# Softmax attention of a two-block network: 36 single-parity steps against 19 steps that take both parities

## The chip, the cores and the metric

The kernel runs on one core of one Trainium2 chip. The metric is the device time of one execution in microseconds. All five engines of the core take part: TensorE (PE) does the products, VectorE (DVE) and ScalarE (ACT) the elementwise work, GpSimd (POOL) the low halves of the weights, SyncE (SP) starts the transfers.

## The reference, cut to what matters

The network is a first block of two layers and a second block of one, over 512 tokens of width 1024. The change touches one stage of the first block, which runs once in each of its two layers: the projection to the 3072 columns `dn_qkv` with its short causal convolution and SiLU, and beside it the softmax attention with a sliding window over 16 query heads and 2 key heads of width 64.

```python
dn_qkv = jax.nn.silu(causal_dwconv(dn_qkv, dn_conv[l]))      # 3072 columns, 4 taps

# swa_sink_attention, in 4 blocks of 128 queries; each sees its own and the previous block of keys
s = jnp.einsum('bnqhgd,bnkhd->bnhgqk', qb, kb) * (D ** -0.5)
s = jnp.where(mask[None, :, None, None], s, -jnp.inf)
m = jnp.maximum(jnp.max(s, axis=-1, keepdims=True), sink)
p = jnp.exp(s - m)
denom = jnp.sum(p, axis=-1, keepdims=True) + jnp.exp(sink - m)
o = jnp.einsum('bnhgqk,bnkhd->bnqhgd', p / denom, vb)
```

## The kernel before, in words

Weights come in slabs of two tiles of 128 columns. For each tile ACT makes a rounded high half (`high`, line 212) and POOL the remainder (`low`, line 216), and `gemm` (line 269) multiplies both with the high and low halves of the activations: 24 matmuls of 512 columns for a tile, 12 of them for the first four depth chunks and 12 for the rest. `high` of tile t + 2 waits until tile t is multiplied. The tiles of this stage take the PSUM banks 0, 1 and 2 in turn.

The stage has 24 such tiles (`QKV_TILES`). VectorE's `conv(t)` reads the finished tile out of its bank in four instructions of 512 columns (lines 971 and 974); it waits for the end of `gemm` of tile t. ScalarE's `silu` follows in groups, after tiles 3, 7, 11, 15 and 19 and at the end.

Between the halves of the tiles lie the steps of the attention. A unit `u` is two query heads of one parity (their 64 rows stand on partitions 0 to 63 or 64 to 127) in one block of queries: 32 units, the first 8 with one block of keys (narrow, 128 columns a head), the other 24 with two (wide, 256 columns a head). A unit goes through

- PE `scores` (line 874): two products into bank 4 or 5, contraction over 64 partitions;
- DVE `before`: scale and mask (line 928), row maximum (932), maximum with the sink, difference, negation (935 to 938);
- ACT `exps` (991, 993): two exponentials with their sums, and the sink's;
- DVE `after`: sum, reciprocal, two scalings (943, 945, 949);
- PE `turn` (885): 2 or 4 transposes into bank 6; ACT `copies` (999) reads them out;
- PE `values` (898): 2 or 4 products with 64 output rows, into bank 3 or 7 (`values_bank`, which alternates with the pair of heads);
- once both parities of a pair are there: ACT `store` (1004) keeps the high half, DVE `keep` (955) the low half, which frees the bank (`a_done`).

Step `u` of PE issues scores of `u`, turn of `u - 3` and values of `u - 4`. ACT's step is exps, copies, store; DVE's is keep, before, after. Each engine works through its own written order, so what a waiting instruction has behind it waits too. `slots(t)` places three steps in two tiles: after the first and the second half of an even tile and after the first half of an odd one; 36 steps in all. On DVE a step after the first half of tile t stands ahead of `conv(t)`, one after the second half stands behind it; on ACT `high(t + 2)` lies between.

The PSUM bank of a pair's values is guarded by

```python
elif u % 2 == 0 and u >= 4:
    pe.wait_ge(a_done, u // 2 - 1)
```

SP's queue loads the remaining slabs of this stage, writes zeros to two arrays in DRAM, and loads the first slabs of the next stage. The stage ends with a barrier of all engines.

Of the kernel before, what the change touches and what calls it, by code (L numbers as in the profile page):

```python
# [12 lines left out]
ACT = mybir.ActivationFunctionType  # L13
# [117 lines left out]
def build(nc, d, out):  # L131
# [4 lines left out]
    with ExitStack() as ctx:  # L136
# [274 lines left out]
        with ExitStack() as st:  # L411
# [147 lines left out]
            with nc.Fori(0, DEPTH) as l:  # L559
# [253 lines left out]
                def values_bank(w):  # L813

                    return ps[7 if w % 2 else 3]

                def stored(w):
                    i, m = w // 4, 2 * (w % 4)
                    return (slice(m, m + 2), slice(i * P, (i + 1) * P),
                            values_bank(w)[:, 0:2 * P].rearrange("p (m t) -> p m t", m=2))  # L820

                NU, LAG, QKV_TILES, SILU = 8, 3, 24, 4
                units = NU * TT

                def width(u):

                    return P if u < NU else 2 * P

                def s1(u):
                    return big[:, 24 + u % 4, :]  # L830

                def turned(u):
                    return big[:, 28 + u % 2, :]

                def st_(u, n, w=2):
                    return big[:, 30, 16 * (u % 4) + 2 * n:16 * (u % 4) + 2 * n + w]

                def two(ap, u):

                    return ap[:, 0:2 * width(u)].rearrange("p (j k) -> p j k", j=2)  # L840

                def slots(t):

                    first = 3 * (t // 2) + (2 if t % 2 else 0)
                    return (first,) if t % 2 else (first, first + 1)

                with nc.Block() as block:  # L847
                    @block.sync
# [16 lines left out]

                    @block.tensor
                    def _(pe):
                        def scores(u):
                            i, w, par = u // NU, u % NU // 2, u % 2
                            if u >= 2:  # L870
                                pe.wait_ge(a_pre, 5 * (u - 2) + 1)
                            for j in range(2):
                                m = 2 * w + j
                                ins = nc.tensor.matmul(ps[4 + u % 2][:, width(u) * j:width(u) * (j + 1)],
                                                       sq[HD * par:HD * par + HD, m, i * P:(i + 1) * P],
                                                       kd[HD * par:HD * par + HD, m // 4, (i + 2) * P - width(u):(i + 2) * P],
                                                       start=True, stop=True)
                            ins.then_inc(a_scored, 1)

                        def turn(u):  # L880
                            pe.wait_ge(a_post, u + 1)
                            if u >= 1:
                                pe.wait_ge(a_tc, u)
                            for n in range(2 * width(u) // P):
                                ins = nc.tensor.transpose(ps[6][:, n * P:(n + 1) * P], s1(u)[:, n * P:(n + 1) * P], ident)
                            ins.then_inc(a_tp, 1)

                        def values(u):
                            i, w, par, nb = u // NU, u % NU // 2, u % 2, width(u) // P
                            pe.wait_ge(a_tc, u + 1)  # L890
                            if u == 0:
                                pe.wait_ge(evacuated[3], use[G_SO + 3])
                            elif u % 2 == 0 and u >= 4:
                                pe.wait_ge(a_done, u // 2 - 1)
                            for j in range(2):
                                g, c0 = (2 * w + j) // 4, P * j
                                for b in range(nb):
                                    ins = nc.tensor.matmul(values_bank(u // 2)[HD * par:HD * par + HD, c0:c0 + P],
                                                           vs[:, i + 2 - nb + b, HD * g:HD * g + HD],
                                                           turned(u)[:, (nb * j + b) * P:(nb * j + b + 1) * P],  # L900
                                                           start=(b == 0), stop=(b == nb - 1))
                            ins.then_inc(a_out, 1)

                        def step(u):
                            if u < units:
                                scores(u)
                            if LAG <= u < units + LAG:
                                turn(u - LAG)
                            if LAG < u <= units + LAG:
                                values(u - LAG - 1)  # L910

                        for t in range(QKV_TILES):
                            gemm(pe, G_QKV + t, (hh, hl), k1=4)
                            step(slots(t)[0])
                            gemm(pe, G_QKV + t, (hh, hl), k0=4)
                            if t % 2 == 0:
                                step(slots(t)[1])

                    @block.vector
                    def _(dve):  # L920
                        def before(u):

                            w, par = u % NU // 2, u % 2
                            dve.wait_ge(a_scored, u + 1)
                            if u >= 4:
                                dve.wait_ge(a_tp, u - 3)
# [31 lines left out]
                        def step(u):  # L958
                            if u >= LAG + 3 and u % 2 == 0:
                                keep((u - LAG - 3) // 2)  # L960
                            if u < units:
                                before(u)
                            if 2 <= u < units + 2:
                                after(u - 2)

                        def conv(t):
                            gt = G_QKV + t
# [8 lines left out]
                                                               ).then_inc(c_tap if s < 3 else evacuated[bank[gt]], 1)  # L976

                        for t in range(QKV_TILES):
                            step(slots(t)[0])
                            conv(t)  # L980
                            if t % 2 == 0:
                                step(slots(t)[1])
                        keep(units // 2 - 1)

                    @block.scalar
                    def _(act):
# [7 lines left out]

                        def copies(u):
                            act.wait_ge(a_tp, u + 1)
                            if u >= 2:
                                act.wait_ge(a_out, u - 1)
                            nc.scalar.activation(turned(u)[:, 0:2 * width(u)], ps[6][:, 0:2 * width(u)], ACT.Copy).then_inc(a_tc, 1)

                        def store(w):
                            m, t, bank_ = stored(w)
                            act.wait_ge(a_out, 2 * w + 2)
                            nc.scalar.activation(o_swa[0][:, m, t], bank_, ACT.Copy).then_inc(a_high, 1)

                        def step(u):
                            if u < units:
                                exps(u)
                            if LAG <= u < units + LAG:
                                copies(u - LAG)  # L1010
                            if LAG < u <= units + LAG and (u - LAG - 1) % 2 == 1:
                                store((u - LAG - 1) // 2)

                        def silu(t):
                            gt = G_QKV + t
# [3 lines left out]
                        high(act, G_QKV)  # L1019
                        high(act, G_QKV + 1)  # L1020
                        for t in range(QKV_TILES):
                            step(slots(t)[0])
                            high(act, G_QKV + t + 2)
                            if t % 2 == 0:
                                step(slots(t)[1])
# [1811 lines left out]
```

## Time and profile before

| | us |
|---|---|
| median of 3 runs (3077.69 to 3086.43) | 3082.3 |
| the profiled execution, its own time | 3085.06 |
| its span in the profile | 3083.2 |
| PE busy in the span | 2745.9 (89%) |
| DVE busy | 1411.5 (46%) |
| ACT busy | 1110.3 (36%) |
| POOL busy | 902.1 (29%) |

The mean granted clock of TensorE is 0.936 of full speed. Times in rows are microseconds from the start of the span unless marked ns. PEld is the load of stationary weights, which overlaps the products. A matmul of plain f32 operands shows as two records; one of the rounded halves and a transpose show as one. The end of a matmul's record is modelled, so that records overlap; the distance from one start to the next is the measure of what a product costs. "idle before <- X" names what the engine waited for.

### The profile page before, as it was taken

What the parts mean: (1) busy time and instruction counts of PE and PEld (TensorE: products, weight loads), DVE (VectorE), ACT (ScalarE), POOL (GpSimd) and SP (SyncE); (2) the same over time, 40 slices, a digit from 0 to 9 for tenths busy, and PEclk for the clock granted to TensorE, in tenths of its full rate; (3) what the DMA queues carried; (4) which work ended last, traced back from release to release, by engine and by line L of the source; (5) the groups of instructions that cost most, each with busy time, mean ns of one, the idle gap of its engine ahead of it and who ended that gap; (6) DMA issues with size and microseconds to landing.
All of it is one profiled execution on the core that took longest, in us unless ns stands there. A gap on an engine that the chain in (4) does not pass through costs nothing. (4 is left out here: it accounts for less than half of the span.)

```text
span 3083.2 us, 34820 instructions
## 1 busy us (share of the span) xinstructions
PE 2745.9 (89%) x12993; PEld 2174.7 (71%) x12993; DVE 1411.5 (46%) x2693; ACT 1110.3 (36%) x1896; POOL 902.1 (29%) x402
## 2 busy tenths in 40 slices
PE   2789999898979999658999989998999987998998
PEld 1567768797858878536776778876788775875676
DVE  4247747654623430233775576453343108624423
ACT  1335455235333321033454532443333213224423
POOL 0342222111424444214222211133344332321242
PEclk6899999899989999869999989999999998988999
DMA  5211313644212322332113265422222225521132
GB/s 171 82 55 55 110 62 108 166 147 143 83 55 96 98 94 93 100 116 69 55 55 110 69 161 178 140 93 68 82 95 95 89 87 135 130 69 35 41 116 82
DMA packets 347832, 299.79 MB, mean 97 GB/s; under 512 B 56910, under 2 KB 335652, under 8 KB 346660
## 3 DMA queue, kind: packets, MB, share of 16 engines
q1 hardware_dynamic: 295716, 279.49, 29.3%
q10 hardware_dynamic: 51968, 18.35, 2.3%
q8 instruction: 90, 1.47, 0.2%
q14 instruction: 58, 0.48, 0.0%
HBM read 267.89 MB, written 29.93 MB: 97 GB/s over the span
## 5 line engine op out<-in xcount | busy, mean ns | idle before, releaser
L269 PE MATMUL ps<-hh,split 128*128 128x512 f32 x3936 | 1352.2, 410 | 97.0 <-POOL split L216 50.5
L216 POOL TENSOR_TENSOR split<-ring,split 128x1024 fp32r<-128x1024 f32 (+2 forms) x342 | 798.6, 2336 | 1724.6 <-ACT split L212 1724.6
L269 PEld LDWEIGHTS ps<-hh,split 128*128 128x128 f32 x3936 | 755.6, 192 | 284.8 <-POOL split L216 71.7
L269 PE MATMUL ps<-hl,split 128*128 128x512 f32 x1968 | 783.0, 398 | 0.0
L212 ACT ACTIVATE split<-ring 128x1024 fp32r<-128x1024 f32 (+2 forms) x342 | 348.4, 1020 | 934.2 <-PE ps L269 719.6
L269 PEld LDWEIGHTS ps<-hl,split 128*128 128x128 f32 x1968 | 379.3, 193 | 74.9 <-issue 7.4
L269 PE MATMUL ps<-split 128*128 128x512 f32 x1152 | 286.4, 406 | 13.0 <-PEq L847 11.1
L269 PEld LDWEIGHTS ps<-split 128*128 128x128 f32 x1152 | 219.3, 191 | 75.0 <-issue 26.8
L1883 PE MATMUL ps<-split 128*128 128x512 f32 x1056 | 243.4, 393 | 9.6 <-PEq L1762 9.6
L1883 PEld LDWEIGHTS ps<-split 128*128 128x128 f32 x1056 | 200.8, 190 | 52.2 <-issue 10.4
L457 DVE SCALAR_TENSOR_TENSOR vs<-ring,c_act,vs 128x256 f32<-128x256 f32 x336 | 179.5, 534 | 6.3
L554 POOL TENSOR_TENSOR split<-ring,split 128x1024 fp32r<-128x1024 f32 x32 | 76.2, 2381 | 361.3 <-ACT split L546 361.3
L991 ACT ACTIVATE big<-big 128x256 f32<-128x256 f32 (+1 forms) x128 | 60.7, 475 | 179.3 <-DVE big L938 179.2
L1896 DVE SCALAR_TENSOR_TENSOR x<-ps,mod,x 128x512 f32 x16 | 12.0, 751 | 234.8 <-PE ps L1883 234.8
L974 DVE SCALAR_TENSOR_TENSOR big<-ps,pv,big 128x511 f32<-128x511 f32 x144 | 107.8, 749 | 5.1
L1807 DVE TENSOR_TENSOR wk<-wk,ps 128x512 f32<-128x512 f32 x44 | 30.3, 688 | 163.3 <-PE ps L269 163.3
L1796 DVE TENSOR_SCALAR wk<-ps,pv 128x512 f32<-128x512 f32 x44 | 33.1, 751 | 111.9 <-PE ps L269 111.9
L475 PE MATMUL ps<-cst,vs 128*128 128x1 f32 x192 | 32.5, 273 | 56.7 <-DVE vs L457 56.2
L971 DVE TENSOR_SCALAR big<-ps,pv 128x512 f32<-128x512 f32 x48 | 36.0, 751 | 91.5 <-PE ps L269 91.5
L475 PEld LDWEIGHTS ps<-cst,vs 128*128 128x128 f32 x192 | 34.6, 238 | 60.9 <-DVE vs L457 57.4
L1799 DVE SCALAR_TENSOR_TENSOR wk<-ps,pv,wk 128x511 f32<-128x511 f32 x88 | 65.9, 749 | 13.7 <-DVE wk L1796 6.2
L1097 DVE TENSOR_TENSOR big<-big,wk 128x512 f32<-128x512 f32 x32 | 39.2, 1225 | 71.4 <-ACT wk L1079 71.4
(370 smaller groups left out, 3339.7 us busy)
## 6 DMA issues: line engine op xcount, KB each, us to landing
ring<-in_w_in_dram SPq DMA_DIRECT2D x60, 1024.0 KB, 5.2
ring<-in_w_up_dram SPq DMA_DIRECT2D x44, 1024.0 KB, 5.1
ring<-in_w_ada_dram SPq DMA_DIRECT2D x64, 512.0 KB, 3.6
ring<-in_w_in_dram SPq DMA_DIRECT2D x34, 512.0 KB, 5.3
ring<-in_w_ada_dram SPq DMA_DIRECT2D x16, 1024.0 KB, 5.3
ring<-in_w_down_dram SPq DMA_DIRECT2D x16, 896.0 KB, 4.7
ring<-in_w_swa_out_dram SPq DMA_DIRECT2D x8, 1024.0 KB, 5.0
ring<-in_w_dn_out_dram SPq DMA_DIRECT2D x8, 1024.0 KB, 5.1
```

The lines of the kernel that those rows point to most:

```text
L212: nc.scalar.activation(halves(pt, nk)[0], slot(n, nk)[:, :, e * P:(e + 1) * P], ACT.Copy).then_inc(high_made, 1)
L216: on.tensor_tensor(halves(pt, nk)[1], slot(n, nk)[:, :, e * P:(e + 1) * P], halves(pt, nk)[0], ALU.subtract).then_inc(low_made, 1)
L269: ins = nc.tensor.matmul(ps[bank[gt]][0:m, :], w[:, k, :], r[:, k, :], start=(k == 0 and w is w_high and r is rhs[0]), stop=(k == nk - 1 a ...
L457: nc.vector.scalar_tensor_tensor(out=acc, in0=w, scalar=c_act[:, k:k + 1], in1=acc, op0=ALU.mult, op1=ALU.add).then_inc(ada_added, 1)
L475: ins = nc.tensor.matmul(out[:, e:e + 1], ada_sum[:, m % 2, e * P:(e + 1) * P], ones[:, 0:1], start=True, stop=True)
L554: nc.gpsimd.tensor_tensor(halves(gt, KD)[1], quarter((gt - G_GB) % 2, KD), halves(gt, KD)[0], ALU.subtract).then_inc(low_made, 1)
L971: nc.vector.tensor_scalar(y, tile[:, :], w[3], None, ALU.mult).then_inc(c_tap, 1)
L974: nc.vector.scalar_tensor_tensor(out=y[:, s:], in0=tile[:, 0:T - s], scalar=w[3 - s], in1=y[:, s:], op0=ALU.mult, op1=ALU.add).then_inc(c_ ...
L991: nc.scalar.activation(half, half, ACT.Exp, bias=st_(u, 2)[:, j:j + 1], accum_out=st_(u, 3)[:, j:j + 1]).then_inc(a_exp, 1)
L1097: nc.vector.tensor_tensor(tile, tile, wk[:, 10 + n % 2, :], ALU.mult).then_inc(n_scaled, 1)
L1799: nc.vector.scalar_tensor_tensor(out=y[:, s:], in0=ps_[:, 0:T - s], scalar=w[2 - s], in1=y[:, s:], op0=ALU.mult, op1=ALU.add).then_inc(u_t ...
L1883: ins = nc.tensor.matmul(ps[bank[gt]][:, :], w[:, k, :], r[:, k0 + k, :], start=(k0 + k == 0 and w is w_high and r is g_high), stop=(k0 + ...
```

## The change

A step now takes both parities of a pair of heads (a double, `v`), 16 doubles in place of 32 units. Within `scores` and `values` the products alternate between the parities, that is, between the two halves of the array: of its rows in `scores` (banks 4 and 5), of its columns in `values`. All values go to bank 3. `turn` writes its transposes to bank 6 or 7 by parity. There are 6 buffers of scores and 4 of turned scores in place of 4 and 2. `LAG` is 2 doubles: step `v` is scores of `v`, turn of `v - 2`, values of `v - 3`. On ACT the copies of the step lead its exponentials; on DVE the order is keep, after (of the double before), before. 19 steps are spread over the 48 halves of tiles: after halves 0, 2, 5, 7, 10, 12, 15, 17 and so on to 45, where an odd number is the end of a tile. The guard of bank 3 is `a_done` of the double before, and that `keep` now stands in DVE's step of the same number as the `values` that waits for it.

```diff
-                NU, LAG, QKV_TILES, SILU = 8, 3, 24, 4
-                units = NU * TT
+                NU, LAG, QKV_TILES, SILU = 8, 2, 24, 4
+                doubles = NU * TT // 2
-                def slots(t):
-                    first = 3 * (t // 2) + (2 if t % 2 else 0)
-                    return (first,) if t % 2 else (first, first + 1)
+                def slots(t, half):
+                    steps = doubles + LAG + 1
+                    return [v for v in range(steps) if v * 2 * QKV_TILES // steps == 2 * t + half]
...
+                        def scores(v):
+                            i, w, n = v // 4, v % 4, width(2 * v)
+                            if v >= 1:
+                                pe.wait_ge(a_pre, 5 * (2 * v - 1) + 1)
                             for j in range(2):
                                 m = 2 * w + j
+                                for par in range(2):
+                                    ins = nc.tensor.matmul(ps[4 + par][:, n * j:n * (j + 1)],
+                                                           sq[HD * par:HD * par + HD, m, i * P:(i + 1) * P],
+                                                           kd[HD * par:HD * par + HD, m // 4, (i + 2) * P - n:(i + 2) * P],
+                                                           start=True, stop=True)
+                                    if j:
+                                        ins.then_inc(a_scored, 1)
+                        def turn(v):
+                            pe.wait_ge(a_post, 2 * v + 2)
+                            if v >= 1:
+                                pe.wait_ge(a_tc, 2 * v)
+                            for u in (2 * v, 2 * v + 1):
+                                for n in range(2 * width(u) // P):
+                                    ins = nc.tensor.transpose(ps[6 + u % 2][:, n * P:(n + 1) * P], s1(u)[:, n * P:(n + 1) * P], ident)
+                                ins.then_inc(a_tp, 1)
+                        def values(v):
+                            i, w, nb = v // 4, v % 4, width(2 * v) // P
+                            pe.wait_ge(a_tc, 2 * v + 2)
+                            if v == 0:
                                 pe.wait_ge(evacuated[3], use[G_SO + 3])
+                            else:
+                                pe.wait_ge(a_done, v)
...
                                 for b in range(nb):
+                                    for par in range(2):
+                                        ins = nc.tensor.matmul(ps[3][HD * par:HD * par + HD, c0:c0 + P],
...
-                        def step(u):
-                            if u >= LAG + 3 and u % 2 == 0:
-                                keep((u - LAG - 3) // 2)
-                            if u < units:
-                                before(u)
-                            if 2 <= u < units + 2:
-                                after(u - 2)
+                        def step(v):
+                            if LAG + 2 <= v:
+                                keep(v - LAG - 2)
+                            if 1 <= v <= doubles:
+                                after(2 * v - 2)
+                                after(2 * v - 1)
+                            if v < doubles:
+                                before(2 * v)
+                                before(2 * v + 1)
...
+                            if LAG <= v < doubles + LAG:
+                                copies(2 * (v - LAG))
+                                copies(2 * (v - LAG) + 1)
+                            if v < doubles:
+                                exps(2 * v)
+                                exps(2 * v + 1)
+                            if LAG < v <= doubles + LAG:
+                                store(v - LAG - 1)
```

## Rows read from the trace of the kernel before

**Rows 1.** The page's busy time, share of the span and instructions, by engine.
```profile
PE 2745.9 (89%) x12993; PEld 2174.7 (71%) x12993; DVE 1411.5 (46%) x2693; ACT 1110.3 (36%) x1896; POOL 902.1 (29%) x402
```

**Rows 2.** Windows, both layers' stage; length, busy PE, PEld, DVE, ACT, POOL; clock, DMA.
```profile
195.77:418.49 222.72, 218.22 (x1040) 162.60 (x1040) 151.70 (x395) 102.39 (x260) 57.23 (x24) 0.99 0.24 76
1455.08:1677.84 222.76, 218.25 (x1040) 162.70 (x1040) 151.72 (x395) 102.39 (x260) 57.21 (x24) 0.99 0.24 76
```

**Rows 3.** Timeline of PE: a tile, a wide step, half a tile; start, length, records.
```profile
280.77 0.50 PE L269 MATMUL ps<-hh,split 128*128 128x512 f32 x1
...
286.46 1.13 PE L874 MATMUL ps<-kd,sq 64*128 64x256 f32 x4
287.51 0.66 PE L885 MATMUL ps<-cst,big 128*128 128x128 f32 x4
288.10 1.09 PE L898 MATMUL ps<-big,vs 128*64 128x128 f32 x8
289.12 0.50 PE L269 MATMUL ps<-hh,split 128*128 128x512 f32 x1
...
292.06 1.13 PE L874 MATMUL ps<-kd,sq 64*128 64x256 f32 x4
```

**Rows 4.** Timeline of PE, one narrow step.
```profile
230.96 0.71 PE L874 MATMUL ps<-kd,sq 64*128 64x128 f32 x4
231.60 0.44 PE L885 MATMUL ps<-cst,big 128*128 128x128 f32 x2
231.97 0.65 PE L898 MATMUL ps<-big,vs 128*64 128x128 f32 x4
232.55 0.50 PE L269 MATMUL ps<-hh,split 128*128 128x512 f32 x1
```

**Rows 5.** Timeline of PE in the second block, products that alternate between halves.
```profile
2652.44 2.67 PE L2231 MATMUL ps<-b_uc,b_drive_w 128*64 128x64 f32 x84
...
2681.53 0.66 PE L2248 MATMUL ps<-b_w_c,b_read_w 64*128 64x63 f32 x8
2682.12 0.66 PE L2243 MATMUL ps<-b_uc,x 128*128 128x64 f32 x4
2682.71 0.66 PE L2248 MATMUL ps<-b_w_c,b_read_w 64*128 64x63 f32 x8
```

**Rows 6.** Waits of PE in the first layer's stage: us in total, times, longest.
```profile
PE ps L885 <- ACT big L999: 4.2, 7, 1.2
```

**Rows 7.** Timeline of DVE: a wide unit's before and after, a tile's conv, a keep.
```profile
287.62 0.69 DVE L928 SCALAR_TENSOR_TENSOR big<-ps,cst 128x512 f32<-128x512 f32 x1 [0.67 <-PE ps L874]
...
289.41 0.15 DVE L943 TENSOR_TENSOR big<-big 128x2 f32<-128x2 f32 x1
...
289.80 0.61 DVE L949 TENSOR_SCALAR big<-big 128x256 f32<-128x256 f32 x2
...
292.17 0.75 DVE L971 TENSOR_SCALAR big<-ps,pv 128x512 f32<-128x512 f32 x1 [1.76 <-PE ps L269]
...
295.19 0.42 DVE L955 TENSOR_TENSOR split<-ps,split 128x256 fp32r<-128x256 f32 x1
```

**Rows 8.** Timeline of ACT: a silu group between its tables, then exps, copy, store.
```profile
265.21 1.28 ACT L1017 ACT_TABLE_LOAD   x1
...
268.70 1.28 ACT L991 ACT_TABLE_LOAD   x1
...
289.54 0.51 ACT L991 ACTIVATE big<-big 128x256 f32<-128x256 f32 x1 [4.63 <-DVE big L938]
...
290.63 0.58 ACT L999 ACTIVATE big<-ps 128x512 f32<-128x512 f32 x1
291.11 0.37 ACT L1004 ACTIVATE split<-ps 128x256 fp32r<-128x256 f32 x1
```
**Rows 9.** Windows around an idle time of PE in the second block; columns as in Rows 2.
```profile
2932.03:2935.38 3.35, 0.00 (x0) 0.03 (x1) 1.93 (x2) 1.15 (x2) 1.26 (x1) 1.00 0.03 7
2935.38:2938.79 3.41, 3.41 (x8) 2.76 (x9) 2.06 (x3) 0.00 (x0) 0.00 (x0) 0.50 0.90 305
```

More of the change, by code:

```diff
@@ L811, in build, with stored @@
                 zeros = big[:, 30:32, :].rearrange("p a c -> p (a c)")[:, 2 * P:2 * P + ZERO]
[L813 to L818, printed above, removed]
+                def stored(v):
+                    i, m = v // 4, 2 * (v % 4)
                     return (slice(m, m + 2), slice(i * P, (i + 1) * P),
[L820 to L823 removed]
+                            ps[3][:, 0:2 * P].rearrange("p (m t) -> p m t", m=2))
+                NU, LAG, QKV_TILES, SILU = 8, 2, 24, 4
+                doubles = NU * TT // 2
                 def width(u):
@@ L873, in scores @@
                                 m = 2 * w + j
[L874 to L891, printed above, removed]
+                                for par in range(2):
[5 more added lines that the diff above has]
+                                        ins.then_inc(a_scored, 1)
@@ L897, in values @@
                                 for b in range(nb):
[L898 to L901, printed above, removed]
-                            ins.then_inc(a_out, 1)
-                        def step(u):
-                            if u < units:
[L906 to L910, printed above, removed]
+                                    for par in range(2):
+                                        ins = nc.tensor.matmul(ps[3][HD * par:HD * par + HD, c0:c0 + P],
+                                                               vs[:, i + 2 - nb + b, HD * g:HD * g + HD],
+                                                               turned(2 * v + par)[:, (nb * j + b) * P:(nb * j + b + 1) * P],
+                                                               start=(b == 0), stop=(b == nb - 1))
+                            ins.then_inc(a_out, 1)
+                        def step(v):
+                            if v < doubles:
+                                scores(v)
+                            if LAG <= v < doubles + LAG:
+                                turn(v - LAG)
+                            if LAG < v <= doubles + LAG:
+                                values(v - LAG - 1)
                         for t in range(QKV_TILES):
                             gemm(pe, G_QKV + t, (hh, hl), k1=4)
-                            step(slots(t)[0])
+                            for v in slots(t, 0):
+                                step(v)
                             gemm(pe, G_QKV + t, (hh, hl), k0=4)
-                            if t % 2 == 0:
-                                step(slots(t)[1])
+                            for v in slots(t, 1):
+                                step(v)
                     @block.vector
@@ L978, in _ @@
                         for t in range(QKV_TILES):
-                            step(slots(t)[0])
+                            for v in slots(t, 0):
+                                step(v)
                             conv(t)
-                            if t % 2 == 0:
-                                step(slots(t)[1])
-                        keep(units // 2 - 1)
+                            for v in slots(t, 1):
+                                step(v)
+                        keep(doubles - 1)
                     @block.scalar
@@ L996, in copies, with step @@
                             act.wait_ge(a_tp, u + 1)
-                            if u >= 2:
-                                act.wait_ge(a_out, u - 1)
-                            nc.scalar.activation(turned(u)[:, 0:2 * width(u)], ps[6][:, 0:2 * width(u)], ACT.Copy).then_inc(a_tc, 1)
+                            if u >= 4:
+                                act.wait_ge(a_out, u // 2 - 1)
+                            nc.scalar.activation(turned(u)[:, 0:2 * width(u)], ps[6 + u % 2][:, 0:2 * width(u)], ACT.Copy
+                                                 ).then_inc(a_tc, 1)
                         def store(w):
                             m, t, bank_ = stored(w)
-                            act.wait_ge(a_out, 2 * w + 2)
+                            act.wait_ge(a_out, w + 1)
                             nc.scalar.activation(o_swa[0][:, m, t], bank_, ACT.Copy).then_inc(a_high, 1)
[L1006 to L1012, printed above, removed]
+                        def step(v):
+                            if LAG <= v < doubles + LAG:
+                                copies(2 * (v - LAG))
+                                copies(2 * (v - LAG) + 1)
+                            if v < doubles:
+                                exps(2 * v)
+                                exps(2 * v + 1)
+                            if LAG < v <= doubles + LAG:
+                                store(v - LAG - 1)
                         def silu(t):
@@ L1021, in _ @@
                         for t in range(QKV_TILES):
-                            step(slots(t)[0])
+                            for v in slots(t, 0):
+                                step(v)
                             high(act, G_QKV + t + 2)
-                            if t % 2 == 0:
-                                step(slots(t)[1])
+                            for v in slots(t, 1):
+                                step(v)
                             if t % SILU == SILU - 1 and t + 1 < QKV_TILES:
```

19 lines of the change are left out of this document (6 added, 13 removed).

## The prediction, before the run

> **What bounds the kernel now.** I read the page first: PE is busy for 89% of the span and no other engine for half of it [rows 1]. Then the windows of the stage that the change touches. It lasts 222.7 us in each layer, 445.5 us in all, at a granted clock of 0.99; PE is busy for 218.2 of the 222.7, DVE for 151.7, ACT for 102.4 [rows 2]. So the stage is a queue of products, and what counts is how long PE's program takes and what it waits for. The table of waits names one wait of PE inside it: turns that wait until ACT has copied the transposes before them, 4.2 us in 7 times [rows 6]. The reader should see that whatever else is on DVE and ACT is at present covered.
>
> The timeline of PE gives the prices by distance of starts. A tile with a step behind it takes 286.46 - 280.77 = 5.69 us and half a tile 292.06 - 289.12 = 2.94, so a bare half is 2.75, a tile 5.50, and the passage into and out of a step costs 0.19. A wide step takes 1.05 for scores, 0.59 for turn and 1.02 for values, 2.66 together [rows 3]; a narrow one 0.64 + 0.37 + 0.58 = 1.59 [rows 4].
>
> **Products of two halves.** The trace of before has no attention product that alternates, but the second block has products that do. At L2231 84 records of 64 columns, alternating between the column halves, take 2.67 us, 0.22 of it the tail of the last: 0.03 us a record. At L2248, alternating between the row halves, eight records of 63 columns take 2682.12 - 2681.53 = 0.59 us, 0.07 a record, while the whole-array products at L2243, with as many columns, need 2682.71 - 2682.12 = 0.59 for four, 0.15 a record [rows 5]. Values in one half take 1.02 / 8 = 0.13 a record of 128 columns [rows 3], which is four times 0.03 for twice the columns. Both point to two halves at work at once. I bound the price of a pair by that of one product (full overlap) and that of two (none), and take the first, since the two nearest rows both show it. In between: if the two records of a product must pass before the other half joins, each group ends half a product later, 0.26 for wide scores and 0.13 for values, about 10 us over both layers.
>
> **PE's work after.** A wide double: scores 1.05 (four products in the time of two), turn with 8 transposes, values 1.02. Four transposes take 0.59 and two 0.37 [rows 3, 4], so one more is 0.11 and eight are 1.03. Together 3.10, against 5.32 for two steps before: 2.22 less, and 0.19 for a passage saved, 2.41. Twelve of them: 28.9 us. A narrow double: 0.64 + 0.59 + 0.58 = 1.81 against 3.18, so 1.37 + 0.19 = 1.56, four times: 6.2. There are 19 steps for 36, 17 passages fewer, of which 16 are counted; the last is 0.2. Sum for one layer: 35.3 us.
>
> **Waits that go.** The turn now comes two steps behind its scores and one whole step, some 10 us, behind the copies that free the banks, and it has two banks. A silu group with its tables takes 269.98 - 265.21 = 4.8 us on ACT [rows 8], less than a step's distance. The 4.2 us [rows 6] go.
>
> **Waits that come.** `values(v)` waits for `a_done` of double `v - 1`, and that `keep` is the first thing in DVE's step of the same number. Six of the steps with a guarded bank and scores stand at the end of a tile (halves 15, 17, 25, 27, 35, 37). There DVE has `conv` ahead of the step, and `conv` can't begin before that tile is multiplied. Let S be the start of scores. Conv begins at S + 0.11 and the keep behind it at 295.19 - 292.06 = S + 3.13; it takes 0.42 [rows 3, 7], so the bank is free at about S + 3.6 with the handover. PE is ready for values at S + 1.05 + 1.03 = S + 2.08. It waits 1.5 us, six times: 9.0. Behind the wait PE holds the next gemm, nobody else's. The last step, after half 45, has only values in it: PE is ready at once and waits 3.5. In the steps after a first half PE has another 2.75 us of gemm, arrives at 4.9 and more after the tile's end, and the keep is done at 3.6: no wait, as long as DVE starts its conv in time.
>
> The 3.5 us may drop the clock. In the second block PE stood idle for 3.35 us, and for the next 3.41 us the granted clock was 0.50, the 1.2 GHz level [rows 9]; that costs 1.7 us. I take it once a layer. For the six waits of 1.5 I take nothing: the seven waits of up to 1.2 in the present stage left it at 0.99 [rows 2, 6].
>
> A rule of the Trainium skill bears on these waits. It says that packing the array speeds up TensorE but not the emptying of PSUM, which may become the bottleneck (TensorEngine Tiling (Array Packing), Performance Considerations, PSUM Bottleneck). The six waits are a mild form of it; the strong form is the second rival below.
>
> **DVE and ACT.** DVE's work is moved, not changed. A wide unit's before is 289.41 - 287.62 = 1.79, its after 290.41 - 289.41 = 1.00, conv 3.02 [rows 7]. A double is 2 x 2.79 + 0.42 = 6.0. The pattern repeats after five tiles and four steps: DVE 5 x 3.02 + 4 x 6.0 = 39.1 us, PE 5 x 5.50 + 4 x 3.29 + 2 x 1.5 = 43.7 (before: 27.5 + 7.5 x 2.85 = 48.9). So DVE goes from 80% to 89% full and stays covered, with 4.6 us in hand. ACT: exps of a unit 290.63 - 289.54 = 1.09, copy 0.48, store 0.37 [rows 8], 3.5 for a double: far from full. Its new order delays exponentials to DVE's `before`, which is later than the copies anyway; the `after` that needs them comes a step later. Where a step stands ahead of `high`, ACT reaches it at about S + 8 (keep by 0.9, after 2.0, before 3.6, exps 1.1, store 0.4); the gemm that needs it begins at S + 3.3 + 2.75 + 5.5 + 3.3 = S + 14.8, which leaves over 6 us for both halves' making. SP's queue has its transfers unchanged, paced by `low`; I cost it at nothing.
>
> **The sum.** For a layer 35.3 + 4.2 - 9.0 - 3.5 - 1.7 = 25.3 us, for two 50.6. The profiled execution took 3085.06, so 3034.5; it stood 2.8 above the median, on which basis it is 3031.7. I predict 3031.
>
> **The rivals.**
> - No overlap (the change doesn't do what it says): a wide double costs 2.10 + 1.03 + 2.04 = 5.17, a narrow one 1.28 + 0.59 + 1.16 = 3.03. Each saves 0.34 with its passage: 5.7 us a layer, plus 4.2, less six waits of 0.5, less 5.2 at the end: 1.7 a layer, 3079. Against it stand both row and column pairs [rows 5]. What differs here is only the number of columns. Chance 0.07.
> - Emptying PSUM on DVE weighs more than I say: if DVE is 1.5 us late at every keep (queued behind a late before, or an instruction that waits for ACT), the six waits double to 3.0, the last becomes 5, and the first-half steps begin to wait 0.2. That is 12.5 more a layer: 3056. DVE at 89% of its time speaks for it, the 4.6 us in hand against it. Chance 0.17. This is where the page's rule would lead.
> - Slower: DVE becomes the bound. It decides from a double of (48.9 - 15.1) / 4 = 8.45 us on DVE, where I have 6.0; at 9.0 the five tiles take 51.1 us, 2.2 more than before, 4.8 times in each of two layers: 3103. It needs 2.45 us of idle time within each step, which could come only from ACT's exponentials arriving after DVE's `after` is due. They end some 2.5 us after `before`, and `after` comes after at least one conv. Chance 0.05.
> - No new waits to speak of, all work saved: 39.5 a layer, 3003. The code's order is against it. Chance 0.08.
>
> My forecast has 0.63, with its own range 3018 to 3045: the stagger above (10 us up), the clock falling in some of the short waits (1.7 each), no clock loss at the end (3.4 down), and the phase of later clock changes, which the shift of all that follows may move by a few us either way.
>
> **Range and chances.** 3010 to 3062 takes in the second rival and leaves out about 0.2: the full gain, the missing overlap, the slow case. About 0.3%, 9 us, is what can be told from no change. Faster than 3073: the first, second and fourth cases and my own, 0.88; same: no overlap, 0.07; slower: VectorE as the bound, 0.05.
>
> **What would show it.** In the profile after: the scores of a wide double (L874's successor, 8 records) from start to start with turn 1.05 us and values 1.02; turns without a wait for ACT; PE waiting for the keep before values 1.5 us in six places a layer and 3.5 once; the stage 197 us long, DVE busy for the same 151 us in it. I am wrong if the pairs cost like two, if PE's wait also stands in the first-half steps, or if DVE has no idle time left.

## The result, and the profile after

The changed kernel takes 3035.76 us (median of 4 runs, 3035.06 to 3043.63), the kernel before 3083.57 (4 runs, 3077.69 to 3086.43): a ratio of 0.9853, 95% interval 0.9831 to 0.9875. I had predicted 3031. The profiled execution took 3035.43 us, 49.6 less than before; the sum of the prediction was 50.6.

The page's busy times of the changed kernel, in the form of [rows 1]:

```profile
PE 2673.0 (88%) x12993; PEld 2132.2 (70%) x12993; DVE 1435.8 (47%) x2693; ACT 1103.7 (36%) x1892; POOL 904.8 (30%) x402
```

PE is busy for 73 us less. DVE is busy for 24 us more, with the same number of instructions; I had priced no such growth. Windows over the two stages of the changed kernel, from the first gemm's start to the last one's end as in [rows 2]:

```profile
195.58:400.91 205.33, 187.91 (x1040) 146.42 (x1040) 165.34 (x395) 100.11 (x259) 57.19 (x24) 0.96 0.26 83
1428.59:1632.01 203.42, 186.91 (x1040) 145.96 (x1040) 164.34 (x395) 100.25 (x259) 57.14 (x24) 0.96 0.26 84
```

The stages lost 17.4 and 19.3 us, 36.8 together, where 50.6 were predicted. PE is idle for 17.4 and 16.5 us in them, against 4.5 before, and the granted clock fell from 0.99 to 0.96. The other 12.8 us came from outside the stage (below). So the total was nearly right, but the place was not.

The timeline of PE in the changed kernel at a step after the end of a tile (compare [rows 3]):

```profile
301.32 1.13 PE L871 MATMUL ps<-kd,sq 64*128 64x256 f32 x8
302.38 1.09 PE L884 MATMUL ps<-cst,wk 128*128 128x128 f32 x8
305.17 1.09 PE L898 MATMUL ps<-wk,vs 128*64 128x128 f32 x16 [1.69 <-DVE split L956]
306.19 0.50 PE L269 MATMUL ps<-hh,split 128*128 128x512 f32 x1
```

Scores of both parities take 1.06 us, values 1.02: each pair of products has the price of one, as forecast. Between turn and values lie 2.79 us where 1.03 is work: the wait for the keep (L956). The table of PE's waits in the first stage (us, times, longest; the 6.1 us for POOL stands before the first tile and was there before):

```profile
PE ps L898 <- DVE split L956: 13.8, 8, 3.6
PE ps L269 <- POOL split L216: 6.8, 2, 6.1
PE ps L898 <- ACT wk L1003: 2.9, 2, 2.1
```

The waits of turn for ACT's copies [rows 6] are gone. New are 13.8 + 2.9 + 0.7 = 17.4 us instead of the predicted 12.5. Three of these waits, of 0.8 to 0.9 us each, stand in steps after a first half (values at 236.2, 245.9 and 291.9 us), where the prediction had none. Two things in the trace lie behind the difference. First, DVE's sum of two 128x2 operands in `after`. All its instances, then the timeline of DVE and of POOL around one:

```profile
L944 DVE TENSOR_TENSOR big<-big x64: 149/155/2359, 207.9 to 1602.8; 128x2 f32<-128x2 f32 x64
```
```profile
290.95 2.36 POOL L216 TENSOR_TENSOR split<-ring,split 128x1024 fp32r<-128x1024 f32 x1 [7.89 <-ACT split L212]
...
291.68 1.65 DVE L944 TENSOR_TENSOR big<-big 128x2 f32<-128x2 f32 x1
293.36 0.17 DVE L946 RECIPROCAL big<-big 128x2 f32<-128x2 f32 x1
```

The median is 155 ns and the longest 2359. The one shown begins at 291.68 and ends at 293.33; POOL's instruction ends at 293.31. 29 of the 64 began while POOL ran, and each of them ended 0.01 to 0.02 us after POOL's instruction; 27 of them took more than 0.2 us. Before, 2 of 64 did.

Second, the clock. Windows of the changed kernel behind a wait of 2.1 us and behind the last wait, of 3.6 us:

```profile
317.40:320.80 3.40, 3.40 (x9) 2.63 (x9) 3.19 (x11) 0.00 (x0) 0.10 (x1) 0.50 0.57 169
392.50:396.00 3.50, 3.35 (x20) 2.82 (x21) 0.01 (x1) 0.38 (x1) 0.11 (x1) 0.52 0.02 5
```

The clock fell to the 1.2 GHz level for 3.4 us three times in the first stage: after waits of 2.12, 2.08 and 3.62 us, not after those of 1.52 to 1.69. In the second stage it fell after a wait of 2.10 us, but not after one of 2.09, and after the last, of 3.62, for 6.8 us. So the length of a wait alone does not say whether the clock falls.

### The profile page after: what moved, and what is told of

The parts are those of the page before. It is cut to its first block and busy times, and to the rows that moved or that the text cites. A ratio compares the mean times of both kernels' runs of the same rounds, so it can differ in the third digit from the quotient of the medians.

```text
span 3033.6 us, 34778 instructions
## 1 busy us (share of the span) xinstructions
PE 2673.0 (88%) x12993; PEld 2132.2 (70%) x12993; DVE 1435.8 (47%) x2693; ACT 1103.7 (36%) x1892; POOL 904.8 (30%) x402
## 5 line engine op out<-in xcount | busy, mean ns | idle before, releaser
L269 PE MATMUL ps<-split 128*128 128x512 f32 x1152 | 285.4, 405 | 10.4 <-PEq L843 8.5
L995 ACT ACTIVATE big<-big 128x256 f32<-128x256 f32 (+1 forms) x88 | 41.5, 473 | 94.7 <-DVE big L939 94.7
L1819 DVE TENSOR_TENSOR split<-wk,split 128x512 f32 (+1 forms) x44 | 66.9, 1520 | 9.9 <-ACT split L1845 9.9
```

The lines of the kernel that those rows point to most:

```text
L269: ins = nc.tensor.matmul(ps[bank[gt]][0:m, :], w[:, k, :], r[:, k, :], start=(k == 0 and w is w_high and r is rhs[0]), stop=(k == nk - 1 a ...
L995: nc.scalar.activation(half, half, ACT.Exp, bias=st_(u, 2)[:, j:j + 1], accum_out=st_(u, 3)[:, j:j + 1]).then_inc(a_exp, 1)
L1819: nc.vector.tensor_tensor(g_low[:, ds(j + 4 * i, 1), :], wk[:, 8 + j % 4, :].unsqueeze(1), g_high[:, ds(j + 4 * i, 1), :], ALU.subtract).t ...
```

## The experiments

"Stages" is the sum of both layers' stages measured as above, from the profiled execution; "ratio" is against runs of the kernel before taken together with it. What lies outside the stages varied between 2621 and 2635 us among the changed kernels, though their instructions there are the same but for POOL's where its work was cut or split, so differences of a few us are read from the stages. The stage lengths in the expectations count the idle time behind the last tile too, 4.25 us in the changed kernel (205.33 there is 209.6).

| kernel | stages, us | median, us | ratio (95%) |
|---|---|---|---|
| before | 445.5 | 3083.6 | |
| changed | 408.7 | 3035.8 | 0.9853 (0.9831 to 0.9875) |
| sum without tensor_tensor | 405.9 | 3041.4 | 0.9861 (0.9843 to 0.9879) |
| keep ahead of conv | 395.1 | 3023.2 | 0.9811 (0.9785 to 0.9837) |
| no alternation | 415.6 | 3048.6 | 0.9877 (0.9860 to 0.9893) |
| exponentials first | 414.4 | 3041.6 | 0.9852 (0.9836 to 0.9869) |
| sum and keep | 392.4 | 3024.8 | 0.9799 (0.9783 to 0.9816) |
| quarter of POOL's work | 392.6 | 3020.2 | 0.9781 (0.9765 to 0.9797) |
| scores apart | 409.5 | 3035.7 | 0.9841 (0.9821 to 0.9861) |
| first halves only | 405.1 | 3035.1 | 0.9828 (0.9812 to 0.9844) |
| POOL in four parts | 402.5 | 3032.0 | 0.9836 (0.9806 to 0.9866) |
| four parts, keep ahead | 389.3 | 3020.7 | 0.9788 (0.9757 to 0.9819) |
| the same, scores apart | 392.3 | 3027.7 | 0.9817 (0.9785 to 0.9848) |
| keep ahead, before first | 367.8 | 2999.3 | 0.9730 (0.9701 to 0.9759) |

### Does the alternation save the time?

```diff
-for j in range(2):
-    for par in range(2):        # scores; values likewise
+for par in range(2):
+    for j in range(2):
```

> The changed kernel with the products of a double in the order of before: all of one parity, then all of the other, in scores and in values. Everything else stays. Theory (two halves work at once only when neighbours in the queue alternate): wide scores take 2.1 us instead of 1.07 and wide values 2.0 instead of 1.02, 24.9 + 4.9 us a layer, of which the waits at tile ends take back 1 us in six places: +23 a layer, 3083, about the time of before. Rival (the gain came from fewer passages and the new order of the other engines, or one parity behind the other overlaps too): within 5 us of 3035.8.

The theory fell: the stages grew by 3.4 us a layer, not 23. The timeline of PE in this kernel at the same step:

```profile
302.39 1.14 PE L871 MATMUL ps<-kd,sq 64*128 64x256 f32 x8
303.46 1.09 PE L884 MATMUL ps<-cst,wk 128*128 128x128 f32 x8
306.08 1.55 PE L898 MATMUL ps<-wk,vs 128*64 128x128 f32 x16 [1.53 <-DVE split L956]
```

Scores take 1.07 us though the parities no longer alternate. In the trace the first record of the second parity starts 0.01 us after the first of the first, though three records stand between them in the program, and the semaphore events of the two parities' ends lie 0.06 us apart: PE starts a product of the idle half past those that wait for the busy one. In values, with eight records of a parity, it reaches only so far: four start alone, the fifth to eighth pair with the first four of the other parity, whose last four follow alone; from start to the next gemm 1.48 us instead of 1.02. Twelve wide doubles a layer at 0.46 are 5.5 us, and the stages are 3.4 us a layer longer, since the waits at tile ends take a part back. So alternation is worth 3 to 4 us a layer, all of it in values. The medians differ by 12.8 us; the rest of that lies outside the stages. That the scores of both parities stand next to each other is what the other gain needs, and the next run parts them.

```diff
 if v < doubles:
-    scores(v)
+    scores(v, 0)
 if LAG <= v < doubles + LAG:
     turn(v - LAG)
+if v < doubles:
+    scores(v, 1)
```

> The changed kernel with the scores of the two parities parted by the turn of the step, so that whole-array transposes lie between the two halves' products and no queue order can let them overlap; values as in the changed kernel. The run without alternation had shown scores of 1.07 us either way. Theory (the halves' products overlap whenever they are near each other in PE's queue, and that overlap is what saves time): the scores of a wide double now take 2.1 us, 12 x 1.15 + 4 x 0.75 = 16.8 us a layer, of which 6 waits at tile ends take back 1.1 each: +10 a layer, 3056. Rival (the halves do not work at once, the records only look so): no more than 2 us a layer for the extra passages, 3040.

The timeline, the window and the waits of PE in the first stage of this kernel:

```profile
299.70 1.13 PE L870 MATMUL ps<-kd,sq 64*128 64x256 f32 x4
300.76 1.09 PE L882 MATMUL ps<-cst,wk 128*128 128x128 f32 x8
301.78 1.13 PE L870 MATMUL ps<-kd,sq 64*128 64x256 f32 x4
303.39 1.09 PE L896 MATMUL ps<-wk,vs 128*64 128x128 f32 x16 [0.48 <-DVE split L956]
304.41 0.50 PE L269 MATMUL ps<-hh,split 128*128 128x512 f32 x1
```
```profile
194.65:399.33 204.68, 197.97 (x1040) 152.75 (x1040) 163.59 (x396) 100.41 (x260) 56.83 (x24) 0.98 0.26 83
```
```profile
PE ps L896 <- DVE split L956: 6.5, 7, 3.6
```

Parted, the scores do cost 2.1 us, so the overlap is real. But the total did not move. That is the rival's time without the rival's reason: PE is busy for 10 us more in the stage (197.97 against 187.91) and waits that much less. The waits inside the stage fell from 17.4 to 6.5 us, the six at tile ends from 1.5 to 2.1 us to 0.5, and the clock drops behind the waits of 2 us went (the stage's mean clock is 0.98). In the changed kernel the overlap of scores gave nothing that arrived at the end.

### The wait for the keep

```diff
 for v in slots(t, 0):
     step(v)
+for v in slots(t, 1):
+    if LAG + 2 <= v:
+        keep(v - LAG - 2)
 conv(t)
 for v in slots(t, 1):
-    step(v)
+    step(v, True)               # without its keep
```

> The changed kernel with one thing moved: where a step stands at the end of a tile, DVE's keep goes ahead of that tile's conv instead of behind it. Theory: values waits for a keep that is queued behind conv; the waits of 1.5 to 2.2 us in six places a layer and of 3.8 in the last go, with the clock drops that follow them; that is up to 18 us a layer, but DVE (about 41.6 us of work in five tiles with its waits for POOL) then bounds PE (40.7), so 10 us a layer, 3016. Rival: DVE as a whole is already the bound and the wait only moves to turn or to gemm: less than 3 us a layer, 3030 or more.

The window of its first stage:

```profile
196.10:393.81 197.71, 183.20 (x1040) 142.67 (x1040) 167.34 (x396) 99.66 (x260) 56.95 (x24) 0.99 0.27 86
```

It takes 7.6 and 6.1 us a layer less than the changed kernel, more than the rival's 3 and less than the theory's 10. The keep behind conv is one cost. DVE is now busy for 167 of 198 us, and PE still waits 14 us, in first-half steps too.

> The changed kernel with the 19 steps placed after first halves of tiles only (one or no step a tile, five tiles without), so that every keep that values waits for lies behind the conv of the tile before and never behind one that is just being finished. Theory (the wait behind conv is the cost): waits of 1.5 to 3.8 us and the clock drops behind them go, up to 15 us a layer; but four or five tiles in a row with a step give DVE 9.0 us of work and its waits for POOL against PE's 8.8, so a part comes back as waits of turn or values: 9 us a layer less, 3018, like the run with the keep ahead of conv. Rival (DVE needs the longer distances of 2 and 3 halves): within 4 us of 3035.8 or slower.

The edit is in `slots`: `v * QKV_TILES // steps == t and half == 0`. The waits of PE in its first stage, without the one ahead of the first tile:

```profile
PE ps L269 <- POOL split L216: 10.4, 5, 2.9
PE ps L898 <- DVE split L956: 3.7, 4, 1.8
```

It takes 1.8 us a layer less. The waits for the keep fell from 13.8 to 3.7 us, but gemm now waits 10.4 us for the low halves of the weights. Before the longest of these waits the trace shows the chain: DVE's sum is held for 1.5 us, its `before` ends late, ACT's exponentials wait 4.7 us for it, and ACT's `high`, which stands behind them, starts at 232.60; `low` follows at 233.72 and gemm at 236.13. The theory had the sign, not the size, and not this path.

### DVE and POOL

```diff
-nc.vector.tensor_tensor(st_(u, 4), st_(u, 3), st_(u, 1), ALU.add)
+nc.vector.tensor_scalar(st_(u, 4)[:, 0:1], st_(u, 3)[:, 0:1], st_(u, 1)[:, 0:1], None, ALU.add)
+nc.vector.tensor_scalar(st_(u, 4)[:, 1:2], st_(u, 3)[:, 1:2], st_(u, 1)[:, 1:2], None, ALU.add)
```

> The changed kernel (3035.8 us) with DVE's sum of two 128x2 columns sets in after() made by two tensor_scalar additions in place of one tensor_tensor. In the changed kernel this tensor_tensor takes 0.60 us on average instead of 0.17 and in 29 of 64 cases ends together with the POOL instruction that ran when it began. Theory: it waits for POOL, and the lateness of DVE that follows adds to PE's waits: the mean falls back to 0.1 to 0.2 us, DVE's busy time falls by some 24 us, the waits of the first-half steps (0.97 and 0.91 us) go and the waits at tile ends shrink to 1.5 to 1.6; 4 to 6 us a layer less, 3025. Rival: DVE's lateness is covered and only the keep behind conv counts: DVE's time falls all the same, the total stays within 3 us of 3035.8.

> The changed kernel with both edits: the sum as tensor_scalar and the keep ahead of conv at tile ends. Theory that the two costs are separate (keep behind conv, and DVE kept by POOL): DVE has 39.1 us of work in five tiles and PE 40.7, so most of the new waits go: 18 us a layer less, 3000. Rival (DVE's chain sets the pace anyway): not below the better of the two single edits by more than 3 us.

Groups of DVE in the kernel with the sum alone (the scaling had a mean of 332 ns in the changed kernel):

```profile
L952 DVE TENSOR_SCALAR big<-big 128x256 f32<-128x256 f32 (+1 forms) x88 | 38.5, 479 | 1.5
...
L944 DVE TENSOR_SCALAR big<-big 128x1 f32<-128x1 f32 x64 | 13.1, 204 | 0.0
```

Inconclusive as a test: a good part of the wait did not go, it moved to the scaling (332 to 479 ns, some 9 us a layer), and the two additions of 0.2 us cost some 8 us a layer more than one sum that is not held, so DVE's time stayed. Each lengthened scaling of the first stage began while POOL ran and ended 0.08 us (128 columns) or 0.15 us (256 columns) after POOL's instruction. With the keep ahead as well, it is 1.3 us a layer better than the keep alone, as the rival had it; the 18 us a layer of the theory did not come.

```diff
-low(pool, G_QKV + t)
+# the same tensor_tensor on depth chunks 0 and 1 of 8 only
```

> The changed kernel with POOL's instruction for the low half of the weights of this stage cut to 2 of 8 depth chunks (the other chunks keep what lay in their buffer, so the projection is not the reference's); nothing else is changed. The POOL instruction takes about 0.7 us instead of 2.4. Theory (DVE's small tensor_tensor waits for the end of the POOL instruction that runs when it begins): the excess of DVE's busy time, 16 to 17 us a layer, falls to 5 or less, the waits of the two first-half steps near 1 us each and the parts of the tile-end waits above 1.6 go: 3 to 6 us a layer less, 3027. Rival (DVE's lateness is covered): DVE's time falls, the total stays within 3 us.

The window of its first stage, the waits of PE in it, and the sum's group:

```profile
194.59:390.94 196.35, 183.23 (x1040) 143.72 (x1040) 149.60 (x395) 100.93 (x260) 17.83 (x25) 0.98 0.27 87
```
```profile
PE ps L902 <- DVE split L960: 12.8, 7, 3.6
```
```profile
L948 DVE TENSOR_TENSOR big<-big 128x2 f32<-128x2 f32 x64 | 9.8, 153 | 0.0
```

This kernel leaves out three quarters of this stage's low halves of the weights, so it is a measuring kernel only. It is the decisive run. With POOL mostly out of the way the sum takes 153 ns again and DVE 149.6 us instead of 165.3. PE waits seven times, 12.8 us: six times 1.53 and once 3.6, exactly the places and about the size that the prediction had (12.5). The stage takes 196.35 us; 222.7 - 25.3 = 197.4 was predicted. The theory's 3 to 6 us a layer were too low: it is 9.0 and 7.1, of which some 0.6 comes from the first tile: gemm waits 4.5 us for POOL ahead of it instead of 6.1 and reaches the first scores 0.6 us sooner.

```diff
-low(pool, G_QKV + t)
+for k in range(0, KD, 2):       # all chunks, two at a time; low_made after the last
+    ins = nc.gpsimd.tensor_tensor(w_low[:, k:k + 2, :], ..., ALU.subtract)
```

> The changed kernel (3035.8 us, stages of 209.6 and 207.7) with POOL's instruction for a tile's low half in this stage cut into four of a quarter each; all the work is done. Theory (a DVE instruction with both inputs in SBUF waits for the end of the one POOL instruction that is running, not for POOL's work as a whole): the excess of DVE's time falls from 16 or 17 us a layer to about a quarter, 4 to 5, and the stage goes to 202, close to the 200.6 of the run with a quarter of POOL's work; 3023. Rival (DVE waits until POOL's queue is empty, or the parts cost POOL so much more that PE waits for them): excess and time as before, or slower.

Groups of DVE, the scaling and the sum:

```profile
L956 DVE TENSOR_SCALAR big<-big 128x256 f32<-128x256 f32 (+1 forms) x88 | 36.3, 453 | 1.5
L950 DVE TENSOR_TENSOR big<-big 128x2 f32<-128x2 f32 x64 | 20.5, 320 | 0.0
```

The sum's mean fell by half (602 to 320 ns), but now the scalings wait too (332 to 453): 25 or 26 of the 64 in a layer meet one of POOL's parts. DVE's busy time fell only from 165.3 to 163.3 us. The stages are 3 us a layer shorter, half of what was expected: cutting POOL's work spreads the wait instead of taking it away.

> The changed kernel with POOL's instruction in four parts and, at tile ends, the keep ahead of conv. Theory (the two costs together are what lies between the changed kernel and PE's own work): PE's work alone gives 228.3 - 39.5 = 188.8 us a stage; DVE has 39.1 us and some 1 us of waits for POOL in five tiles against PE's 40.7, so 192 a stage, 3003. Rival (DVE at 96% of its time can't keep up, its waits for PE and ACT come on top): no better than 200 a stage, 3020, as with the keep ahead alone.

> The kernel with POOL's instruction in four parts and the keep ahead, and besides the scores of the two parities parted by the turn, so that they can't overlap. On the changed kernel parting them cost nothing (3035.7). Theory (the overlap saved PE's time there too, but the waits for the keep and for POOL's port took it back): with those waits gone parting costs its work, 12 x 1.15 + 4 x 0.75 = 16.8 us a layer, less what DVE had made PE wait, so 10 to 17 a layer above the kernel without it, 3003 becomes 3023 to 3037. Rival (the halves' overlap is worth nothing in itself): within 4 us of the kernel with the two edits.

The windows of the first stage, one kernel each:

```profile
197.46:392.14 194.68, 183.52 (x1040) 142.75 (x1040) 163.85 (x395) 99.72 (x259) 68.22 (x96) 0.99 0.28 87
```
```profile
197.31:393.41 196.10, 195.79 (x1040) 151.23 (x1040) 163.68 (x396) 99.96 (x260) 67.49 (x96) 0.99 0.28 87
```

Both theories missed. The pair gives 9.7 us a layer, not 16, and 3020.7 us, where its rival stood; DVE still spends 163.9 us. Parting the scores costs 1.5 us a layer here, not 10, and the stages grow by 3.0 us in all, within the rival's 4, but not for its reason: the first kernel's PE is idle for 11 of 194.7 us, the second's for 0.3 of 196.1. That second number is a floor: without the overlap of scores PE's own work fills 196 us.

### Another place for the sum

```diff
 # DVE's step, with the keep ahead of conv as above
-if 1 <= v <= doubles: after(2 * v - 2); after(2 * v - 1)
 if v < doubles: before(2 * v); before(2 * v + 1)
+if 1 <= v <= doubles: after(2 * v - 2); after(2 * v - 1)
```

> The kernel with the keep ahead of conv (3023.2, stages of 202), and in DVE's step before() of the double ahead of after() of the one before. The exponentials start 2 us earlier and the sums of after() come 3.6 us later. Theory (which DVE instruction meets a running POOL instruction depends on its place; behind before() it stands past POOL's 2.4 us): DVE's excess falls from 19 us a layer to 10 or less, 3 to 5 us a layer gained, 3015. Rival (another of DVE's instructions with two SBUF inputs, the maximum with the sink or the difference, meets POOL in its place): excess and time within 3 us of 3023.

The window of the first stage, the waits of PE in it, and DVE's groups of the maximum with the sink and of the sum:

```profile
196.17:380.11 183.94, 182.00 (x1040) 142.74 (x1040) 151.50 (x395) 100.95 (x259) 57.54 (x25) 0.98 0.29 92
```
```profile
PE ps L898 <- DVE split L956: 1.7, 2, 1.1
```
```profile
L936 DVE TENSOR_TENSOR big<-big,sink 128x2 f32<-128x2 f32 x64 | 15.4, 241 | 2.2
...
L944 DVE TENSOR_TENSOR big<-big 128x2 f32<-128x2 f32 x64 | 10.0, 156 | 0.0
```

The stage takes 183.9 us, 38.8 less than before; the prediction's work and old waits came to 39.5. PE is idle for 1.9 of it, DVE busy for 151.5, as before the change. This beats the theory's 3 to 5 us a layer by far: 13.8 less than with the keep ahead alone. It is the fastest kernel of all, 2999.3 us, 87 below the kernel before. Two things changed with the order, the place of the sum and the earlier exponentials; the runs do not part them, though DVE's 16 us alone would be enough. And 183.9 lies 12 us under the floor of 196 without overlap: here, at last, the overlap of the scores reaches the end.

### The order on ACT

The edit puts `exps` back ahead of `copies`.

> The changed kernel (3035.8 us) with ACT's order of before: in a step the exponentials, then the copies of the turned scores. The copies then end about 9 us after the start of the step's scores instead of 3, and the turn that waits for them stands 9.9 us or more after it. Theory (the order on ACT is worth little, the margin of 1 us is eaten up where DVE is late or a silu group lies between): 2 to 4 us a layer more, 3041. Rival (the copies ahead of the exponentials are what lets the doubled step run): 8 us a layer more or worse, 3052 or more. Second rival: no difference, within 3 us.

The stages are 1.8 and 3.8 us longer than the changed kernel's, as the theory had; the ratio, 0.9852, can't tell it from the changed kernel. In this order turn waits for ACT's copies again, 1.8 and 1.5 us in the first stage. The copies' lead is worth 2 to 4 us a layer.

## Why the prediction was right, and where it was not

- **Products of two halves**: right. 1.06 and 1.02 us for wide scores and values. The bound of no overlap and the stagger of 10 us are out. But scores do not need alternating neighbours, as I had assumed, and values need them only for a part.
- **PE's work after, 35.3 us a layer, and the 4.2 of old waits**: right; the last experiment reaches 38.8 of 39.5.
- **Waits that come**: the mechanism and its seven places were right, the size too low. I had 12.5 and got 17.4 us in the first stage. Without POOL's interference it is 12.8. I had called it a sign of being wrong if PE's wait also stood in first-half steps; it did, three times, 2.6 us in all, and these waits went with POOL's work. I priced `after` at 1.00 us a unit from a row [rows 7] in which no POOL instruction ran beside it, and took DVE's work as moved, not changed. In the new place 27 of 64 sums were held by POOL; DVE is busy for 15 to 16 us a layer more than with a quarter of POOL's work.
- **The clock**: one drop a layer forecast, three in the first stage. The other two followed waits of 2.1 us, one for the keep behind a late conv, one for ACT's copies behind exponentials that had waited for DVE. At most 1.7 us each.
- **DVE and ACT**: wrong for DVE. "DVE's work is moved, not changed" is the step that failed, and DVE was not busy for the same 151 us in the stage but for 165: 39.1 us in five tiles left out what the new neighbours cost. The second rival had the effect, DVE late at its keeps, with 12.5 us a layer and no cause. It came to about half: the term is 7 us a layer in the stage.
- **The sum**: 25.3 a layer predicted for the stage, 17.4 and 19.3 measured. Outside the stage 12.8 us went (2637.7 to 2624.9 of span), for which I had only "a few us either way". 2.6 of them are the idle time behind the last tile, 5.56 us before and 4.25 after in each layer. A further part is clock: the stretches at half clock outside the stages add up to 386 us before and 361 after, and 24 us less of them is worth at most 12 (an estimate from these sums). The windows around one slow stretch of the next stage, before and after:

```profile
560.00:580.00 20.00, 13.64 (x52) 12.46 (x53) 11.05 (x32) 2.74 (x4) 3.91 (x2) 0.58 0.71 170
```
```profile
539.50:552.80 13.30, 5.82 (x22) 5.34 (x23) 8.57 (x27) 1.54 (x2) 3.94 (x2) 0.62 0.65 140
```

At 0.58 of 20 us the clock was halved for 17 us, at 0.62 of 13.3 for 10. The instructions behind the idle time are the same, and fewer of them ran at half clock. Why the slow stretches came out shorter is not shown. So the total came out within 1 us of the sum partly by luck: 14 us too little in the stage, 13 unforeseen outside. (The prediction's list of the faster cases names the first rival, which it also counts as no change; the figure 0.88 is that of the second, the fourth and my own.)

## What to carry to other kernels

When instructions are moved, price them beside their new neighbours: a DVE instruction of 0.15 us that reads SBUF twice lasted here until the POOL instruction it met had ended. Look for work that the waiting engine itself holds up (here keep stands behind a conv that can't start before PE has finished the tile): whatever PE saves between the two, it then waits. Read the fully freed version first: until the last wait was gone, half of the saved work was invisible, and parting the scores even looked free.

## What the runs showed of the hardware that I had not expected

- DVE's tensor_tensor with both inputs in SBUF, 128x2, took up to 2.36 us beside POOL's tensor_tensor of 2.4 us and ended with it; 0.15 alone. DVE's tensor_scalar of 128x256, SBUF to SBUF, waits too: its mean rose from 332 to 479 ns when the sum was made otherwise. The Trainium skill states this (SBUF — State Buffer, SBUF: two separate sides: the port pair that DVE and GpSimd share is held for a whole instruction, by a DVE instruction in a 2-port mode or with two SBUF inputs). The trace agrees: the sum of two SBUF inputs was held to the end of POOL's instruction, 2.36 us. I had not weighed it.
- PE started products for an idle half of the array past products of the busy half that stand before them in the program: in scores two products, four records, ahead (0.01 us apart), in values only with the fifth record.
- The granted clock fell to 0.50 for 3.4 us after idle times of 2.08, 2.10 and 2.12 us, and did not after 2.09 and 1.69. In the kernel with POOL's work in four parts it fell after 1.89 us, in the one with the exponentials first it did not after 2.67.
